# A feed-forward's eleven quads in chunks of 3, 4 and 4 instead of 4, 3 and 4

## The chip, the cores and the metric

The kernel runs on one core of one Trainium2 chip. The time is the device time of the program in microseconds; the time before is the median of three runs.

The engines are called as the profile calls them: PE is the matrix engine TensorE (PEld is its weight load), DVE is VectorE, ACT is ScalarE, POOL is GpSimd, SP is SyncE, which issues most of the loads.

## The reference

One layer for 512 prompt tokens and 32 sample tokens: a feed-forward at half weight, a mixer of two linear attentions, a cross attention, and a second feed-forward at half weight. Only the two feed-forwards matter here:

```python
x = x + 0.5 * _swiglu(_rmsnorm(x, w['ffn1_norm_g']), w['ffn1_w_gate'], w['ffn1_w_up'], w['ffn1_w_down'])
...
x = x + 0.5 * _swiglu(_rmsnorm(x, w['ffn2_norm_g']), w['ffn2_w_gate'], w['ffn2_w_up'], w['ffn2_w_down'])

def _swiglu(x, wg, wu, wd):
    return (jax.nn.silu(x @ wg) * (x @ wu)) @ wd
```

x has 544 rows of 1024; gate and up are 1024 x 2816, down is 2816 x 1024, all in float32.

## The kernel before

**Quads and chunks.** The 2816 hidden columns are 22 blocks of 128. Two blocks m = 0, 1 make a quad, so there are eleven. A list `CHUNKS` (line 340) groups the quads: an entry is the first block of the chunk and its number of quads. In a chunk of nq quads, quad t takes the blocks k0 + t and k0 + t + nq. When a chunk's gates and ups are done, its part of the down product is made and added to x, for four pairs of output blocks.

**Jobs.** `JOBS` (lines 341 to 352) is the list that sets the order of all engines: for each feed-forward and chunk the gate and the up of each quad, then the gate of the next chunk's first quad, then four downs. Before, a feed-forward's 34 jobs are: gate and up of four quads, gate of chunk 1, four downs; up and the rest of chunk 1 (three quads), gate of chunk 2, four downs; up and the rest of chunk 2 (four quads), four downs. Behind the last chunk's ups no gate follows, so its first down stands right behind the up whose result it needs.

**Products.** The first four jobs of a feed-forward (two gates, two ups) are plain matrix products. All others use Strassen's scheme: seven products P1 to P7 instead of eight, on sums and differences of blocks. Each float32 operand is split in a high and a low part, and a product of one block takes three matmuls (high by high, low by high, high by low) of 128 x 128 by 272 columns. Gates and ups have four blocks to sum over in a product (12 matmuls), a down has as many as its chunk has quads: 12 matmuls in a chunk of four, 9 in a chunk of three. `half_size` (line 404) gives this size. `SEQ` is the list of all products in order; P3 of a job comes behind P1 of the next.

**Who makes what for a product.** SP loads a job's five weight blocks into `slots`, ten of them, five a job (lines 548 to 566), as soon as the job two before has been split. Two of the five (issued at line 554, first of the job) get a second block added by a POOL transfer that accumulates (`add_on_load`, line 657); POOL waits for SP's two first. Both kinds are 256 KB, or 192 KB in a down of three quads. ACT copies the high part into `ring_w` (line 845), DVE subtracts it for the low part (line 1325), mostly for two products at once (`GROUPS`). Two products whose sizes differ are not paired, so on the way into and out of a chunk of three quads the splits are single. Behind the split of P1, DVE adds a slot that the POOL transfer must have filled (line 1333), behind that of P2 another (line 1338).

**Results.** DVE and ACT combine the products of gate and up, and DVE makes h of a quad with its sums (lines 1441 to 1454, 1351). ACT and DVE split h into `hs` (lines 886, 889, 1466), in a part for the sums m < 3 and one for the rest. A down's last block waits for the last quad of its chunk (`h_ready`, line 2346):

```python
if j == nk - 1:
    h_ready(NF // 2 * n + (CHUNKS[c][0] // 2 + CHUNKS[c][1] - 1), m)
```

DVE adds a down's results to x (lines 1398, 1409, 1410, 1423, 1437). All PE matmuls of a feed-forward have line 2194, that of their helper.

Of the kernel before, what the change touches and what calls it, by code (L numbers as in the profile page):

```python
# [50 lines left out]
def build(nc, a, o):  # L51

    ctx = ExitStack()
    with ctx:
# [282 lines left out]
        N_PLAIN = 4  # L337
        COMBO = {P1: 0, P2: 2, P3: 1, P4: 6, P5: 3, P6: 5, P7: 4}
        SLOT = {P1: 0, P6: 0, P3: 1, P2: 1, P4: 2, P7: 3, P5: 4, W11: 0, W12: 1, W22: 2, W21: 3}
        CHUNKS = ((0, 4), (8, 3), (14, 4))  # L340
        JOBS = []
        for n in range(2):
            for c, (k0, nq) in enumerate(CHUNKS):
                for t in range(nq):
                    if t or not c:
                        JOBS.append(("gate", n, c, t))
                    JOBS.append(("up", n, c, t))
                if c + 1 < len(CHUNKS):
                    JOBS.append(("gate", n, c + 1, 0))
                JOBS += [("down", n, c, m) for m in range(4)]  # L350
                if c + 1 < len(CHUNKS):
                    pass
# [51 lines left out]
        def half_size(J):  # L404

            return 128 * (CHUNKS[JOBS[J][2]][1] if JOBS[J][0] == "down" else 4)

# [5 lines left out]
        def quad_of(J):  # L413

            return NF // 2 * JOBS[J][1] + CHUNKS[JOBS[J][2]][0] // 2 + JOBS[J][3]

# [85 lines left out]

        LAST_UP = CHUNKS[-1][1] - 1
        mem_k_out = o["mem_k"][0, 0].rearrange("(mb p) h d -> p mb (h d)", p=128)
# [2388 lines left out]
```

## Time and profile before

| | us |
|---|---|
| median of three runs | 1301.96 (1300.91 to 1302.71) |
| the profiled execution | 1297.84 |
| its span, first to last instruction | 1296.0 |
| first feed-forward, jobs of chunk 0's downs to the end of chunk 2's ups | 120.18 to 334.50 |
| PE busy | 1256.2 (97% of the span) |
| DVE busy | 932.5 (72%) |
| ACT busy | 617.1 (48%) |

The profile is of one execution. Its span is that of the core's instructions; the rest of the execution's time lies around it. A row of the timeline gives start, duration, engine, line and operation, and in brackets how long the engine had stood idle before and what ended that. A matmul's duration is longer than the distance to the next one, because they are pipelined; what counts is the distance of their starts. The second feed-forward has the same program as the first.

### The profile page before, as it was taken

The numbers are of one execution on the slowest core, as the hardware profiler recorded it, in microseconds if no ns is written. First come the engines' busy times: TensorE is split into PE (matmuls) and PEld (weight loads), VectorE is DVE, ScalarE is ACT, GpSimd is POOL, SyncE is SP. The second block draws the span as 40 slices with busy tenths as digits, with TensorE's granted clock in tenths as the row PEclk, the third lists the DMA queues.
The fourth block names the chain that finished last, engine by engine and source line by source line (L and its number), as shares of the span: only waits on it lengthen the run. The fifth ranks groups of instructions, "written<-read, shape, count | busy, mean of one in ns | idle before, by whom it ended". The sixth has DMA issues, their size and how long they took to land.

```text
span 1296.0 us, 25334 instructions
## 1 busy us (share of the span) xinstructions
PE 1256.2 (97%) x10321; PEld 1216.5 (94%) x10321; DVE 932.5 (72%) x1326; ACT 617.1 (48%) x962; POOL 196.0 (15%) x184
## 2 busy tenths in 40 slices
PE   7999999999889999999999999999999999999987
PEld 7999999999889999998888899879999999999987
DVE  5988778888793376667766544535698878888885
ACT  6455455555462233345534622324445545645553
POOL 1112222232100000002111000100012222222210
PEclk9999999999899999998999999999999999999988
DMA  6578887888653223324055673541458888798861
GB/s 203 116 158 171 179 171 154 179 189 169 135 118 102 69 80 82 82 82 131 19 132 171 215 244 112 190 176 55 119 124 179 175 177 167 146 199 174 175 125 69
DMA packets 302324, 185.03 MB, mean 143 GB/s; under 512 B 10582, under 2 KB 290368, under 8 KB 302212
## 3 DMA queue, kind: packets, MB, share of 16 engines
q1 hardware_dynamic: 233072, 125.61, 33.8%
q0 software_dynamic: 68976, 57.68, 25.6%
q8 instruction: 81, 1.33, 0.5%
q14 instruction: 31, 0.25, 0.1%
q10 hardware_dynamic: 164, 0.16, 0.0%
HBM read 175.53 MB, written 7.88 MB: 142 GB/s over the span
## 4 chain that ended last, share of the span: by engine, by line
PE 41%; DVE 6%; issue 1%; ACT 1%; DMA 1%; another core or an unknown queue 0%; POOL 0%; SPq 0%; DVEq 0%; ACTq 0%
PE ps L2194 39%; DVE ring_w L1325 2%; PE ps L2697 1%; DMA slots<-in_ffn_w_up 1%; DVE xs_lo L1346 1%; ACT ring_w L845 0%; PE ps L2802 0%; DVE hs L1466 0%; PE ps L2728 0%; DVE hf L1454 0%; DVE hf L1351 0%; DVE xf L1351 0%; DVE hf L1448 0%; DVE xf L1358 0%
## 5 line engine op out<-in xcount | busy, mean ns | idle before, releaser
L2194 PE MATMUL ps<-xs_hi,ring_w 128*128 128x272 f32 x2016 | 382.7, 289 | 3.1 <-DVE ring_w L1325 3.1
L1325 DVE TENSOR_TENSOR ring_w<-slots,ring_w 128x1024 fp32r<-128x1024 f32 (+3 forms) x262 | 273.8, 1046 | 102.3 <-ACT ring_w L845 101.1
L2194 PEld LDWEIGHTS ps<-xs_hi,ring_w 128*128 128x128 f32 x2016 | 316.6, 188 | 3.8 <-DVE ring_w L1325 3.8
L845 ACT ACTIVATE ring_w<-slots 128x1024 fp32r<-128x1024 f32 (+3 forms) x262 | 238.9, 918 | 156.5 <-DVE slots L1333 83.5
L2194 PE MATMUL ps<-xs_lo,ring_w 128*128 128x272 f32 x1008 | 291.7, 289 | 0.0
L2194 PE MATMUL ps<-hs,ring_w 128*128 128x272 f32 x1848 | 242.6, 292 | 10.4 <-DVE hs L1466 7.6
L2194 PEld LDWEIGHTS ps<-hs,ring_w 128*128 128x128 f32 x1848 | 238.3, 192 | 13.0 <-DVE hs L1466 9.0
L2194 PEld LDWEIGHTS ps<-xs_lo,ring_w 128*128 128x128 f32 x1008 | 189.6, 188 | 0.0
L2194 PE MATMUL ps<-xn_hi,w_hi 128*128 128x272 f32 x736 | 155.9, 292 | 1.9 <-DVE w_lo L1290 1.9
L2194 PE MATMUL ps<-xn_hi,w_lo 128*128 128x272 f32 x736 | 153.9, 289 | 0.0
L2194 PE MATMUL ps<-xn_lo,w_hi 128*128 128x272 f32 x736 | 153.4, 288 | 0.0
L784 ACT ACTIVATE w_hi<-raw 128x1024 fp32r<-128x1024 f32 x70 | 73.9, 1056 | 146.6 <-PE ps L2194 146.6
L1290 DVE TENSOR_TENSOR w_lo<-raw,w_hi 128x1024 fp32r<-128x1024 f32 x70 | 85.7, 1225 | 46.7 <-ACT w_hi L784 46.3
L2194 PEld LDWEIGHTS ps<-xn_hi,w_hi 128*128 128x128 f32 x736 | 116.3, 189 | 3.1 <-DVE w_lo L1290 2.2
L2194 PEld LDWEIGHTS ps<-xn_hi,w_lo 128*128 128x128 f32 x736 | 117.0, 190 | 0.0
L2194 PEld LDWEIGHTS ps<-xn_lo,w_hi 128*128 128x128 f32 x736 | 116.2, 189 | 0.0
L2194 PE MATMUL ps<-xe_hi,ring_w 128*128 128x272 f32 x512 | 86.7, 292 | 5.1 <-ACT xe_hi L806 3.2
L657 POOL DMA_DIRECT2D slots<-in_ffn_w_down x48 | 61.5, 1536 | 197.7 <-DMA slots<-in_ffn_w_down 197.7
L868 ACT ACTIVATE parts<-ps 128x272 f32<-128x272 f32 x120 | 47.5, 396 | 91.8 <-PE ps L2194 91.8
L657 POOL DMA_DIRECT2D slots<-in_ffn_w_gate x36 | 46.4, 1552 | 251.9 <-DMA slots<-in_ffn_w_gate 251.9
L2194 PEld LDWEIGHTS ps<-xe_hi,ring_w 128*128 128x128 f32 x512 | 73.4, 191 | 6.0 <-DVE ring_w L1325 5.6
L657 POOL DMA_DIRECT2D slots<-in_ffn_w_up x36 | 46.3, 1547 | 145.7 <-DMA slots<-in_ffn_w_up 145.7
(386 smaller groups left out, 1643.1 us busy)
## 6 DMA issues: line engine op xcount, KB each, us to landing
slots<-in_ffn_w_gate SPq DMA_DIRECT2D x106, 256.0 KB, 3.5
slots<-in_ffn_w_up SPq DMA_DIRECT2D x106, 256.0 KB, 3.5
slots<-in_ffn_w_down SPq DMA_DIRECT2D x80, 256.0 KB, 3.4
raw<-in_w_in SPq DMA_DIRECT2D x30, 512.0 KB, 3.8
slots<-in_ffn_w_gate POOLq DMA_DIRECT2D x36, 256.0 KB, 5.6
slots<-in_ffn_w_up POOLq DMA_DIRECT2D x36, 256.0 KB, 5.5
slots<-in_ffn_w_down POOLq DMA_DIRECT2D x32, 256.0 KB, 5.6
slots<-in_ffn_w_down SPq DMA_DIRECT2D x40, 192.0 KB, 2.7
```

The source lines that it names most:

```text
L657: pool.dma_start(slots[:, b_ + q, 0:128 * nk].rearrange("p (k c) -> p k c", c=128), src, accum_op=ALU.add).then_inc(sem(f"sum_in{J % 2}"), 16)
L784: act.activation(w_hi[u0 % 2][:, :], raw[u0 % 4][:, :], ACT.Copy).then_inc(sem("hi_done"), 1)
L845: act.activation(ring_part(g, 0), sources(g), ACT.Copy).then_inc(sem("prod_hi"), 1)
L868: act.activation(part_of(J, p_), ps[:, x_bank(J), 0:HT], ACT.Copy, scale=-1.0 if p_ == P7 else 1.0)\
L1290: dve.tensor_tensor(w_lo[u0 % 2][:, :], raw[u0 % 4][:, :], w_hi[u0 % 2][:, :].bitcast(F32), ALU.subtract).then_inc(sem("lo_done"), 1)
L1325: dve.tensor_tensor(ring_part(g, 1), sources(g), ring_part(g, 0).bitcast(F32), ALU.subtract)\
L1346: dve.tensor_tensor(xs_lo[:, lo:hi, j, :], xf8[:, lo + 1:hi + 1, :], xs_hi[:, lo:hi, j, :].bitcast(F32), ALU.subtract).then_inc(sem("xs_lo ...
L2194: return pe.matmul(out, lhsT, rhs, start=start, stop=stop, skip_group_check=onto)
L2697: ins = pe.transpose(k_bank(n)[:, k, 128 * mb:128 * mb + 128], kv[K_BUF[b]][:, mb, at_:at_ + 128], ident)
```

## The change

`CHUNKS` gives chunk 0 three quads and chunk 1 four; chunk 2 is the same. All else follows from the list.

```diff
-        CHUNKS = ((0, 4), (8, 3), (14, 4))
+        CHUNKS = ((0, 3), (6, 4), (14, 4))
```

In both kernels jobs 0 to 5 are gate and up of quads 0 to 2, and from job 23 on the jobs are the same (the last up group and downs). Between them: before, gate and up of quad 3, gate of quad 4, four downs of four blocks, ups and gates of quads 4 to 6, gate of quad 7, four downs of three blocks. After: gate of quad 3, four downs of three blocks, ups and gates of quads 3 to 6, gate of quad 7, four downs of four blocks.

DVE around the first down of chunk 0, the rows of the kernel before (hf_98 is the h of a quad, gt the gate, part_101 a product's partial sum):

```order
L1448 TENSOR_TENSOR hf_98<-hf_98,gt 128x816
L1454 TENSOR_TENSOR hf_98<-hf_98 128x544
L1351 SCALAR_TENSOR_TENSOR hf_98<-hf_98 128x272 x2
L1325 TENSOR_TENSOR ring_w<-slots,ring_w 128x2x512
L1333 TENSOR_TENSOR slots<-slots 128x512
L1412 TENSOR_TENSOR gt<-part_101,ps 128x272
L1466 TENSOR_TENSOR hs<-hf_98,hs 128x816
L1325 TENSOR_TENSOR ring_w<-slots,ring_w 128x2x512
L1466 TENSOR_TENSOR hs<-hf_98,hs 128x1088
L1325 TENSOR_TENSOR ring_w<-slots,ring_w 128x2x512
```

DVE at the same place, chunk 0's first down, in the changed kernel:

```order
L1448 TENSOR_TENSOR hf_98<-hf_98,gt 128x816
L1325 TENSOR_TENSOR ring_w<-slots,ring_w 128x384
L1333 TENSOR_TENSOR slots<-slots 128x384
L1454 TENSOR_TENSOR hf_98<-hf_98 128x544
L1351 SCALAR_TENSOR_TENSOR hf_98<-hf_98 128x272 x2
L1325 TENSOR_TENSOR ring_w<-slots,ring_w 128x512
L1412 TENSOR_TENSOR gt<-part_101,ps 128x272
L1466 TENSOR_TENSOR hs<-hf_98,hs 128x816
L1325 TENSOR_TENSOR ring_w<-slots,ring_w 128x2x384
L1466 TENSOR_TENSOR hs<-hf_98,hs 128x1088
L1325 TENSOR_TENSOR ring_w<-slots,ring_w 128x2x384
```

The paired split of 2 x 512 (P1 of the down, P3 of the gate before) became two single ones, of 384 ahead of the sums of h and of 512 behind them. These are the rows that stood at chunk 1's first down before; there the rows above stand now.

POOL's queue of accumulating loads in the first feed-forward, from chunk 0's last up to chunk 1's downs, in the kernel before:

```order
L657 DMA slots<-in_ffn_w_gate 128x4x128 x2
L657 DMA slots<-in_ffn_w_down 128x4x128 x8
L657 DMA slots<-in_ffn_w_up 128x4x128 x2
L657 DMA slots<-in_ffn_w_gate 128x4x128 x2
L657 DMA slots<-in_ffn_w_up 128x4x128 x2
L657 DMA slots<-in_ffn_w_gate 128x4x128 x2
L657 DMA slots<-in_ffn_w_up 128x4x128 x2
L657 DMA slots<-in_ffn_w_gate 128x4x128 x2
L657 DMA slots<-in_ffn_w_down 128x3x128 x8
```

And in the changed kernel:

```order
L657 DMA slots<-in_ffn_w_gate 128x4x128 x2
L657 DMA slots<-in_ffn_w_down 128x3x128 x8
L657 DMA slots<-in_ffn_w_up 128x4x128 x2
L657 DMA slots<-in_ffn_w_gate 128x4x128 x2
L657 DMA slots<-in_ffn_w_up 128x4x128 x2
L657 DMA slots<-in_ffn_w_gate 128x4x128 x2
L657 DMA slots<-in_ffn_w_up 128x4x128 x2
L657 DMA slots<-in_ffn_w_gate 128x4x128 x2
L657 DMA slots<-in_ffn_w_up 128x4x128 x2
L657 DMA slots<-in_ffn_w_gate 128x4x128 x2
L657 DMA slots<-in_ffn_w_down 128x4x128 x8
```

The eight loads of three blocks for the downs stand a gate and an up earlier and those of four blocks come second; SP's queue moves in the same way.

## Rows read from the trace of the kernel before

**Rows 1.** The page: busy time of each engine, and the chain's shares.

```profile
PE 1256.2 (97%) x10321; PEld 1216.5 (94%) x10321; DVE 932.5 (72%) x1326; ACT 617.1 (48%) x962; POOL 196.0 (15%) x184
...
PE 41%; DVE 6%; issue 1%; ACT 1%; DMA 1%; another core or an unknown queue 0%; POOL 0%; SPq 0%; DVEq 0%; ACTq 0%
```

**Rows 2.** Windows of feed-forward one: downs, gates and ups, downs (columns above).

```profile
core 0: us, PE busy (x) PEld busy (x) DVE busy (x) ACT busy (x) POOL busy (x), PEclk, DMA share, GB/s
120.18:164.40 44.22, 44.02 (x350) 43.80 (x349) 36.00 (x49) 22.56 (x32) 10.48 (x9) 1.00 0.84 176
164.40:226.50 62.10, 62.10 (x495) 62.10 (x494) 50.70 (x68) 35.17 (x52) 15.39 (x12) 1.00 0.78 162
226.50:260.70 34.20, 33.94 (x269) 33.72 (x268) 30.12 (x48) 19.17 (x32) 8.30 (x7) 1.00 0.84 181
```

**Rows 3.** Timeline of PE, first downs of chunks 0, 1, 2 (start, us, what).

```profile
120.94 0.54 PE L2194 MATMUL ps<-hs,ring_w 128*128 128x272 f32 x3
121.68 0.65 PE L2194 MATMUL ps<-hs,ring_w 128*128 128x272 f32 x3 [0.20 <-DVE hs L1466]
...
227.00 0.41 PE L2194 MATMUL ps<-hs,ring_w 128*128 128x272 f32 x2
227.67 0.65 PE L2194 MATMUL ps<-hs,ring_w 128*128 128x272 f32 x3 [0.26 <-DVE hs L1466]
...
339.21 1.05 PE L2194 MATMUL ps<-hs,ring_w 128*128 128x272 f32 x3 [3.36 <-DVE hs L1466]
340.84 0.56 PE L2194 MATMUL ps<-hs,ring_w 128*128 128x272 f32 x1 [0.58 <-ACT parts L868]
```

**Rows 4.** Timeline of DVE, before and at the first downs of chunks 0, 1.

```profile
91.47 1.23 DVE L1325 TENSOR_TENSOR ring_w<-slots,ring_w 128x1024 fp32r<-128x1024 f32 x1 [1.60 <-ACT ring_w L845]
...
120.62 1.00 DVE L1466 TENSOR_TENSOR hs<-hf,hs 128x816 fp32r<-128x816 f32 x1
...
218.99 1.23 DVE L1325 TENSOR_TENSOR ring_w<-slots,ring_w 128x1024 fp32r<-128x1024 f32 x1 [1.60 <-ACT ring_w L845]
...
226.62 1.00 DVE L1466 TENSOR_TENSOR hs<-hf,hs 128x816 fp32r<-128x816 f32 x1
```

**Rows 5.** The chain, feed-forward two, behind chunk 1's downs (start, us, what).

```profile
1141.59 0.37 SPq L554
...
1142.00 3.77 DMA slots<-in_ffn_w_up
...
1146.85 5.97 DMA slots<-in_ffn_w_up
...
1155.22 0.45 DVE x L1410
...
1155.81 1.24 PE ps L2194 x8
```

**Rows 6.** Timeline, the load behind chunk 1's downs in both feed-forwards.

```profile
246.78 0.92 SPq L554 DMA_DIRECT2D slots<-in_ffn_w_up  x2
...
257.43 0.69 DVE L1333 TENSOR_TENSOR slots<-slots 128x512 f32<-128x512 f32 x1 [0.44 <-DMA slots<-in_ffn_w_up]
...
1152.91 0.69 DVE L1333 TENSOR_TENSOR slots<-slots 128x512 f32<-128x512 f32 x1 [1.11 <-DMA slots<-in_ffn_w_up]
...
1155.38 0.29 PE L2194 MATMUL ps<-xs_lo,ring_w 128*128 128x272 f32 x1
```

**Rows 7.** Windows behind the last chunk's wait, columns as in rows 2.

```profile
338.00:344.00 6.00, 4.21 (x17) 3.92 (x18) 4.88 (x6) 3.01 (x5) 0.00 (x0) 0.55 0.15 44
344.00:350.00 6.00, 6.00 (x44) 6.00 (x44) 3.21 (x5) 2.35 (x4) 2.57 (x2) 0.88 0.88 185
```

**Rows 8.** Landing times of SP's first loads and POOL's, 60 to 340 us.

```profile
DMA to landing us min/median/max: 2.5/3.3/5.2
DMA to landing us min/median/max: 4.2/5.3/7.9
```

## The prediction

> **What bounds the kernel now.** I read the page's busy times and its chain first: TensorE (PE) is busy for 97% of the span, and work of PE is the largest share of the chain that ended last [rows 1]. So only what makes PE wait, or gives it more or less to do, moves the end. Next I cut the first feed-forward at the borders of its stages [rows 2]. Between 164.40 and 226.50 us PE runs without a gap: 62.10 us for 495 matmuls, which is 62.10 / 495 = 0.1255 us each. A Strassen job of four blocks (7 products x 12 matmuls = 84) therefore takes 84 x 0.1255 = 10.54 us, and a down job of a three-quad chunk (7 x 9 = 63) takes 7.91 us. VectorE (DVE) is busy for 36.00 of 44.22 us (81%) beside the downs of chunk 0 and for 30.12 of 34.20 us (88%) beside the smaller downs of chunk 1 [rows 2]: the smaller job leaves less cover, but DVE still fits.
>
> Then I looked at the places where PE stands still, in PE's own rows. In chunks 0 and 1 there are only two kinds.
>
> First, the first down of a chunk waits for the h of the chunk's last quad, in its last block. In chunk 0, three matmuls start from 120.94, so the next could start at 120.94 + 3 x 0.1255 = 121.32 and starts at 121.68: 0.36 us lost. In chunk 1, two start from 227.00, the next could start at 227.25 and starts at 227.67: 0.42 us lost [rows 3]. The releaser is the same DVE subtraction each time, at 120.62 and 226.62 [rows 4].
>
> Second, the first load after the small downs is late. The weights of the job after chunk 1's downs are loaded by SP and then added to by a POOL transfer. In the second feed-forward the first SP issue stands at 1141.59, SP's pair lands at 1142.00 + 3.77 = 1145.77, POOL's second transfer lands at 1146.85 + 5.97 = 1152.82 [rows 5]. DVE waited 1.11 us for it, so it was ready at 1152.91 - 1.11 = 1151.80: the lead was 10.21 us and the landing took 11.23 [rows 6]. What DVE does next is late, and PE starts at 1155.81 [rows 5] where the matmul before, at 1155.38 [rows 6], allows 1155.51: 0.30 us lost. In the first feed-forward the issue is at 246.78 and DVE was ready at 257.43 - 0.44 = 256.99: again a lead of 10.21 us, a wait of 0.44 us, and no loss on PE [rows 6]. So about 0.8 us of such a wait is covered (1.11 costs 0.30, 0.44 costs nothing).
>
> **The change part by part.** Each part occurs in both feed-forwards; I cost one and double it.
>
> PE's work. Chunk 0's four downs go from 12 to 9 matmuls a product: 4 x 7 x 3 = 84 matmuls less, 84 x 0.1255 = -10.54 us. Chunk 1's four downs go from 9 to 12: +10.54 us. One gate job and one up job (the fourth quad) move from before chunk 0's downs to before chunk 1's, with their loads and DVE work. The sum on PE is 0. The bytes loaded are equal too: in either order four jobs of a feed-forward load 7 x 192 KB instead of 7 x 256 KB, and SP's and POOL's queues hold the same transfers with the 192 KB group earlier.
>
> The wait at the first down. The order rows show DVE's work around chunk 0's first down turning, row by row, into what stands at chunk 1's first down before (single splits of 384, then the first hs subtraction). So chunk 0 should lose 0.42 us where it lost 0.36, and chunk 1 should lose 0.36 where it lost 0.42: +0.06 and -0.06, sum 0. This holds if DVE reaches the new place in the same state as the old one. The new first down is the fourth job after the plain ones, close to the place where DVE is behind and PE waits for it. The row that decides is the split of the second pair of products in the gate job ahead of the downs: at 91.47 DVE has stood idle 1.60 us before it, waiting for ScalarE, and at 218.99, the same place ahead of chunk 1, also 1.60 us [rows 4]. DVE has caught up by then, so I take no lag. From both sides: the wait can shrink by at most 0.42 us, and if the first down met DVE in the state of the last chunk, where no gate job stands between up and down, it would lose far more, 3.36 + 0.58 us [rows 3]; the gate job still stands between here, so I take the near row.
>
> The late load. The small downs now stand in chunk 0, and the same late load should follow them there, ahead of chunk 1's first up: nothing in the first feed-forward, 0.30 us in the second. Chunk 1's downs become full ones, and behind chunk 0's full downs no such wait showed: PE was busy for 62.10 of 62.10 us [rows 2]. Taken away 0.30, put back 0.30, sum 0. Below, it is gone in both places: -0.30 us. Above, from the longest landings seen in this feed-forward, 5.2 us for SP's and 7.9 us for POOL's transfer [rows 8]: with 0.41 us between SP's two issues, 0.3 to POOL's start and 0.8 between its two, 0.4 + 5.2 + 0.3 + 0.8 + 7.9 = 14.6 us, less the lead of 10.21 and the 0.8 that is covered = 3.6 us a feed-forward. I take the middle value because the two places of before are the same job sequence.
>
> A rule is to be weighed here. In the trace the two transfers that follow each other take 3.77 and 5.97 us [rows 5]. The Trainium skill, "DMA: Bandwidth & Descriptors", section "Anatomy of one DMA — SWDGE (gpsimd) path", fits a transfer as some 2.0 us fixed plus bytes over 436 GB/s, which is an estimate of 2.6 us for 256 KB. By it the pair with its issues would land some 6.7 us after the first issue, no load would be late anywhere, and the sum would be -0.3 us; the trace disagrees with it here, and the measurement decides.
>
> What does not move. The last chunk keeps its four quads, its jobs follow in the same order, and its long wait of 3.36 us [rows 3] stays, with the low clock behind it [rows 7].
>
> **Sum.** The profiled execution took 1297.84 us with a span of 1296.0. PE's work -10.54 + 10.54, first downs +0.06 - 0.06, late loads -0.30 + 0.30: 0 in each feed-forward, so 1297.84 again. The median of the three runs is 1301.96, 4.12 us above the profiled one; carried over, the forecast is **1302.0**. What a measurement of this kernel can tell from no change is about 0.2%, 2.6 us.
>
> **The rivals.**
>
> Loads in time. With half the chunk behind it, the queue may be emptier at the new place, and the job after the small downs gets its sums in time: -0.30 us, 1301.7. For it speaks the DMA share of 0.78 in the gate and up stage [rows 2]; against it, that the share was 0.84 beside the downs of either chunk and the lead of 10.21 us comes from PE's pace alone. (The fit of the Trainium skill's page above would also have them in time.)
>
> Loads late, the side on which the change costs. At the new place the loads are issued just after the backlog behind the plain jobs; if SP's and POOL's transfers run into each other there, the landing takes up to 14.6 us. To cost 2.6 us, each feed-forward must lose 0.15 + 1.3 = 1.45 us, so both landings must take over 10.21 + 0.8 + 1.45 = 12.5 us; halfway to the bound, +3.5 us, gives 1305.5. A lesser lateness, up to that point, gives 1302.3 to 1304.6. Against it: two such landings took 10.6 and 11.23 us. Were PE to stop as long as at the last chunk's wait, the clock could fall as well, as it does there.
>
> The clock. After PE's stop of 3.36 us the granted clock of 338 to 344 is 0.55 and of 344 to 350 is 0.88 [rows 7]: the lower level of 1.2 GHz for part of it, where 2.4 is full. That is 6 x 0.45 + 6 x 0.12 = 3.4 us of clock, of which PE stood still for 1.2 + 0.6 us and lost nothing: some 2.5 us of cost, as far as these rows tell. If the shifted stages let the clock stand in both feed-forwards, 5.0 us go, 1297.0; one more such stretch costs 2.5 and gives 1304.5 or more. The stop itself does not change, so I give either little.
>
> That the change does not do what it says is out: the order rows show the 3-block loads moved.
>
> **How the numbers follow.** Exchange without a rest, 1302.0: 0.62. Loads in time, 1301.7: 0.14. Loads somewhat late, up to 1304.6: 0.12. Loads late in both, 1305.5: 0.06. Clock kept, 1297.0: 0.04. Clock lost once more: 0.02. Faster by over 0.2%: 0.04. Within: 0.62 + 0.14 + 0.12 = 0.88. Slower: 0.06 + 0.02 = 0.08. The three runs lie 1.05 us below to 0.75 above their median; since three understate the spread I take 1.75 times that, 1.84 and 1.31. Low end: 1301.96 - 0.30 - 1.84 = 1299.8. High end: 1301.96 + 1.31 + 1.3, the somewhat late loads at half their way, = 1304.6. Outside lie the last three cases and a little of the third.
>
> **What would show it.** Right: two stages of about 34.2 and 44.2 us in the other order, a PE gap of 0.4 us at each first down, and DVE waiting 0.4 to 1.1 us for a load after chunk 0's downs and nowhere after chunk 1's. Wrong: a PE gap of over 1 us behind chunk 0's small downs, DVE without its idle time before the first down, or a stretch of lower clock where there was none.

## The result, and the profile after

The changed kernel takes 1303.92 us (median of 20 runs, 1300.32 to 1307.80); the kernel before, on the same chips, 1300.95 (20 runs, 1298.12 to 1302.72). The ratio is 1.0024, 95% interval 1.0016 to 1.0033: 3.1 us slower, from 2.1 to 4.3. The time is inside the range of the forecast, but no change was forecast, with 0.08 for slower by over 0.2%, and slower by over 0.2% is what came. The runs also lie further apart than those of before.

The profiled execution of the changed kernel took 1302.41 us with a span of 1300.5, against 1297.84 and 1296.0. Its page, to be held against [rows 1]: the same instructions, and PE busy 4.5 us longer (where is said below, at the windows of the whole program).

```profile
PE 1260.7 (97%) x10321; PEld 1220.9 (94%) x10321; DVE 932.8 (72%) x1326; ACT 617.0 (47%) x962; POOL 196.0 (15%) x184
```

The windows of the first feed-forward, cut as in [rows 2] (same columns): the small downs now come first, then ups and gates, then the full downs.

```profile
99.68:135.94 36.26, 34.08 (x269) 33.66 (x268) 29.75 (x48) 20.27 (x34) 9.19 (x8) 1.00 0.80 170
135.94:219.21 83.27, 83.27 (x659) 83.27 (x660) 70.24 (x91) 45.57 (x68) 20.94 (x17) 1.00 0.85 178
219.21:263.43 44.22, 44.02 (x351) 43.80 (x350) 35.84 (x48) 22.58 (x33) 11.00 (x9) 1.00 0.86 178
```

The full downs take 44.22 us as before. The small ones take 36.26 where they took 34.20: 2.06 us more, for the same 269 matmuls. PE's timeline says where. Its first downs of chunks 0 and 1 (as in [rows 3]), and the end of chunk 0's small downs:

```profile
99.68 0.92 PE L2194 MATMUL ps<-hs,ring_w 128*128 128x272 f32 x6
100.85 0.52 PE L2194 MATMUL ps<-hs,ring_w 128*128 128x272 f32 x2 [0.26 <-DVE hs L1466]
...
133.73 0.29 PE L2194 MATMUL ps<-xs_lo,ring_w 128*128 128x272 f32 x1
135.94 1.36 PE L2194 MATMUL ps<-hs,ring_w 128*128 128x272 f32 x9 [1.93 <-DVE x L1410]
...
219.21 1.04 PE L2194 MATMUL ps<-hs,ring_w 128*128 128x272 f32 x7
220.46 0.64 PE L2194 MATMUL ps<-hs,ring_w 128*128 128x272 f32 x3 [0.20 <-DVE hs L1466]
```

From 133.73 the next matmul could start at 133.86 and starts at 135.94: 2.08 us lost. The chain of waits through that place (start, us, what), where [rows 5] had 3.77 and 5.97 for the two landings:

```profile
119.94 0.37 SPq L554
...
120.35 4.86 DMA slots<-in_ffn_w_up
...
125.50 0.78 POOL slots L657
126.28 6.68 DMA slots<-in_ffn_w_up
...
135.36 0.45 DVE x L1410
...
135.94 1.11 PE ps L2194 x7
```

And DVE's timeline at three jobs behind downs (compare [rows 6]): behind the small downs of the first feed-forward, behind the full downs of its chunk 1 (259.85), and behind the small downs of the second feed-forward.

```profile
129.00 1.15 DVE L1325 TENSOR_TENSOR ring_w<-slots,ring_w 128x384 fp32r<-128x384 f32 x2
133.05 0.69 DVE L1333 TENSOR_TENSOR slots<-slots 128x512 f32<-128x512 f32 x1 [2.90 <-DMA slots<-in_ffn_w_up]
...
259.85 0.69 DVE L1333 TENSOR_TENSOR slots<-slots 128x512 f32<-128x512 f32 x1
...
1030.14 0.69 DVE L1333 TENSOR_TENSOR slots<-slots 128x512 f32<-128x512 f32 x1 [0.53 <-DMA slots<-in_ffn_w_up]
```

So the late load moved to chunk 0, as said, and in the first feed-forward it is far later than it was anywhere before: 13.02 us from the first issue (119.94) to the last landing (132.96), where the two places of before had 10.56 and 11.23. In the second feed-forward the same job had its loads after 10.65 us, and PE did not stop.

What else differs between the two profiles is read from windows of the whole program: ahead of the first matmul of the feed-forward, first feed-forward, middle, second feed-forward, rest.

```profile
0.00:15.66 15.66, 8.37 (x53) 7.86 (x54) 4.68 (x9) 7.89 (x13) 3.59 (x10) 1.00 0.93 286
15.66:342.06 326.40, 318.48 (x2497) 316.74 (x2497) 274.06 (x367) 181.71 (x259) 71.99 (x56) 0.99 0.77 161
342.06:916.02 573.96, 562.36 (x4886) 527.27 (x4886) 342.93 (x533) 224.80 (x402) 43.33 (x58) 0.98 0.42 122
916.02:1239.36 323.34, 318.00 (x2497) 316.66 (x2497) 268.90 (x356) 174.71 (x248) 71.98 (x56) 0.99 0.77 161
```

The same cuts in the kernel before give 14.95, 324.26, 572.97 and 322.21 us. The first feed-forward is 2.14 us longer. The start, the middle and the second feed-forward are longer by 0.71, 0.99 and 1.13 us, the rest is 0.47 shorter. A second profile of each kernel (below) shows the 2.14 again, and it shows the start and the second feed-forward to come and go. The middle is longer in the second pair too. There PE does the same 4886 matmuls in 562.36 us of busy time instead of 559.71, at a mean granted clock of 0.98 instead of 0.99: at a lower clock a matmul takes longer, and these 2.65 us are more than half of the 4.5.

### The profile page after: what moved, and what is told of

It reads as the page before. It is cut to its first block, busy times and chain, and to the rows that moved or that the text cites. A ratio compares the mean times of both kernels' runs of the same rounds, so it can differ in the third digit from the quotient of the medians.

```text
span 1300.5 us, 25334 instructions
## 1 busy us (share of the span) xinstructions
PE 1260.7 (97%) x10321; PEld 1220.9 (94%) x10321; DVE 932.8 (72%) x1326; ACT 617.0 (47%) x962; POOL 196.0 (15%) x184
## 4 chain that ended last, share of the span: by engine, by line
PE 76%; DVE 15%; ACT 4%; issue 3%; DMA 1%; another core or an unknown queue 0%; POOL 0%; SPq 0%; DVEq 0%; ACTq 0%
PE ps L2194 73%; DVE ring_w L1325 3%; DVE xs_lo L1346 1%; ACT ring_w L845 1%; PE ps L2697 1%; DMA slots<-in_ffn_w_up 1%; DVE hs L1466 1%; DVE hf L1454 1%; DVE lv_qk L1657 1%; DVE hf L1351 1%; DVE xf L1351 0%; PE ps L2802 0%; DVE hf L1448 0%; DVE xf L1358 0%; DVE xf L1360 0%
```

## Experiments

Two theories. **Instruction theory**: a transfer of 16 KB that brings PE its own next instructions falls into the left loads (SP's first pair, line 554) of the job behind the small downs; any other job has slack for it, this one has none (the kernel before has such a load at 306.27 us: a transfer 2.4 us behind the issue, 5.08 us for the second load, and neither DVE nor PE waited for it). **Chance theory**: the late load was one bad execution and the 3 us lie elsewhere, say in the clock. The trace showed the first theory's transfer in the stretch between the pair's first issue and its last landing (119.94 to 125.21 us, the view of DMA queues), as the one packet of queue 8 (packets, MB, share of 16 engines):

```profile
## 3 DMA queue, kind: packets, MB, share of 16 engines
q1 hardware_dynamic: 2040, 1.02, 66.8%
q0 software_dynamic: 137, 0.06, 9.8%
q8 instruction: 1, 0.02, 1.2%
```

1.2% of 16 engines over 5.27 us is 1.0 us of one engine.

### Both kernels once more

No edit in either.

> The changed kernel once more, unaltered, for a second profiled execution. Instruction theory (a 16 KB transfer of TensorE's own instructions falls into the loads of the job behind chunk 0's downs of the first feed-forward, and that job has no slack): the transfer stands again within 3 us of 122.4 us in the span, the second left load again takes over 4.5 us, the slot sum of line 1333 is again over 2 us late near 130 us, and TensorE again stops for 1.5 to 2.5 us near 134 us; 1303 to 1304.5 us. Chance theory (the late load was one bad execution, and the 3 us lie in the clock): the chain of loads takes 10.3 to 11.5 us this time, TensorE loses under 1 us there, and the time is 1303 to 1304.5 us all the same.

> The kernel before once more, unaltered: a second profiled execution, and a comparison of the kernel with itself. Both theories: ratio 1.0000, its interval within 0.9990 to 1.0010. Instruction theory: the jobs behind its three-quad downs (near 250 and 1150 us) again have their sums at most 1.2 us late, since no instruction transfer falls into their left loads, and TensorE loses at most 0.6 us at each. Chance theory: lateness there differs from the first profile by over 1 us in one of the two.

Measured: changed kernel 1.0020 (1.0008 to 1.0031) of the kernel before; the kernel before against itself 1.0004 (0.9993 to 1.0014). The changed kernel's median, 1302.13 us, lies under the 1303 to 1304.5 expected; the kernel before took 1300.19 beside it. Each one's second profile, first feed-forward and middle (changed, then before):

```profile
15.78:342.19 326.41, 318.70 (x2498) 316.81 (x2498) 273.93 (x367) 181.69 (x259) 71.99 (x56) 0.99 0.77 161
342.19:915.48 573.29, 562.51 (x4885) 527.51 (x4885) 342.86 (x533) 224.93 (x402) 43.32 (x58) 0.98 0.42 122
```

```profile
15.85:340.11 324.26, 318.27 (x2497) 316.75 (x2497) 274.08 (x367) 181.78 (x259) 72.01 (x56) 0.99 0.77 162
340.11:911.95 571.84, 559.11 (x4885) 523.97 (x4885) 342.66 (x533) 224.82 (x402) 43.43 (x58) 0.99 0.42 122
```

326.40 and 326.41 against 324.26 and 324.26. The chain at the late job was 13.02 us again, the transfer stood 2.5 us behind the first issue again (2.4 the first time), PE stopped 1.92 us. In the kernel before the same job took 10.43 us this time (10.56). The chance theory falls for the first feed-forward. The second feed-forward took 322.14 and 321.78 us, so most of the 1.13 us more of the first pair of profiles was not the change's. The middle, 573.29 against 571.84 us, is 1.45 us longer this time; what that can mean is said with the clock, further down.

### The change in one feed-forward only

The list was given a second level, one entry for each feed-forward.

```diff
-        CHUNKS = ((0, 3), (6, 4), (14, 4))
+        CHUNKS = (((0, 3), (6, 4), (14, 4)), ((0, 4), (8, 3), (14, 4)))
```

The other kernel has the two entries exchanged.

> Chunks of 3, 4 and 4 in the first feed-forward, 4, 3 and 4 in the second. Instruction theory: the whole cost is in the first feed-forward (2.09 us at the job behind chunk 0's downs, 0.4 us won back at chunk 1): +2 to +3.3 us, ratio 1.0015 to 1.0027. Clock theory: half of the cost, +1 to +2 us, ratio 1.0008 to 1.0015.

> Chunks of 4, 3 and 4 in the first feed-forward, 3, 4 and 4 in the second. Instruction theory: the second feed-forward showed a chain of loads of 10.65 us and no stop of TensorE there, against 0.30 us lost before: -0.4 to +0.4 us, ratio 0.9997 to 1.0003. Clock theory: half of the cost, +1 to +2 us, ratio 1.0008 to 1.0015.

Measured: first feed-forward alone 1.0024 (1.0012 to 1.0036), second alone 1.0000 (0.9987 to 1.0013). By the medians the whole cost is in the first; the two intervals alone would just allow a half in each, but the first feed-forward took 326.33 us with the first changed and 324.53 with the second. The profile of the one with the second changed is not that quiet, though: PE stopped 2.32 us behind its small downs, which was not expected, in an execution 2 us above that kernel's median. So in the second feed-forward the late load comes in some of the profiles; in the first it was there in every profile that had the small downs first and no added instructions.

### Other addresses

Behind the small downs the changed kernel loads columns from block 6 on, the kernel before from block 14 on. Here the chunks exchange weights (the quad numbers follow by count).

```diff
-        CHUNKS = ((0, 3), (6, 4), (14, 4))
+        CHUNKS = ((0, 3), (14, 4), (6, 4))
```

> Chunks of 3, 4 and 4 as changed, but the second and third chunk exchange the weights they read: the job behind chunk 0's small downs loads columns from block 14 on, as the one behind the three-quad downs of the kernel before does, and not from block 6 on. Instruction theory: the same as the changed kernel, chain of loads 12.5 to 13.5 us at that job of the first feed-forward, TensorE stopped 1.6 to 2.3 us, ratio to before 1.0015 to 1.0035. Address theory: chain 10.3 to 11.2 us, stop under 0.6 us, ratio 0.9990 to 1.0010.

Measured: 1.0028 (1.0014 to 1.0041); chain 14.25 us, PE stopped 3.16 us, the transfer 2.8 us behind the issue. The address is not the cause. Chain and stop are above the 12.5 to 13.5 and 1.6 to 2.3 us expected, so the instruction theory did not give their size; here the load ahead was late as well (2.0 us into the pair, in the table below).

### A semaphore of its own for each added load

If the cost is the sum's wait and nothing else, it goes when the sum waits only for what it reads. Line 1333 reads the slot of the first POOL load, yet its semaphore counted both. ScalarE's split of P5 reads the same slot and gets the same semaphore. Two semaphores used once each later in the kernel were merged with neighbours to make room (not shown).

```diff
-    accum_op=ALU.add).then_inc(sem(f"sum_in{J % 2}"), 16)
+    accum_op=ALU.add).then_inc(sem(f"sum{q}_in{J % 2}"), 16)
...
-    act.wait_ge(sem(f"sum_in{J % 2}"), 32 * ((nth(J) + 1) // 2))
+    act.wait_ge(sem(f"sum{4 if p_ == P5 else 3}_in{J % 2}"), 16 * ((nth(J) + 1) // 2))
...
-    dve.wait_ge(sem(f"sum_in{J % 2}"), 32 * ((nth(J) + 1) // 2))
+    dve.wait_ge(sem(f"sum4_in{J % 2}"), 16 * ((nth(J) + 1) // 2))
```

> The changed kernel with a semaphore for each of the two adding loads on POOL's queue, so that the sum of line 1333 waits for the first of them alone (it reads only that one's slot), and the split of P7 for the second. In the profile of the changed kernel the first landed at 129.89 us, the second at 132.96, VectorE was free at 130.15. Late-load theory (the whole cost is this sum's wait): the sum starts within 0.3 us of VectorE being free, TensorE's stop of 1.92 us goes or falls under 0.5 us, and the kernel takes 1.5 to 2.2 us less than the changed kernel: ratio to before 0.9997 to 1.0012. If instead the second load is needed almost as early by the split of P7, a stop of 1 to 2 us moves to the product of P7 and the ratio stays 1.0012 to 1.0030.

> The kernel before with the same two semaphores. In its profile the sum behind the three-quad downs was 0.44 and 1.11 us late, which cost TensorE nothing and 0.30 us. Late-load theory: 0 to 0.5 us faster, ratio 0.9995 to 1.0003. Where it costs elsewhere (the waits on merged semaphores later in the kernel): up to 1.0010.

> The kernel before with the two semaphores, the same file as in the earlier run, for a narrower interval: 0.9988 [0.9975, 1.0001] there. Late-load theory: its profile had no stop of TensorE behind the three-quad downs, where the kernel before had lost 0 and 0.30 us, so at most 0.5 us of gain, ratio 0.9995 to 1.0003. If the gain of the first run is real, 0.9980 to 0.9995.

Measured: changed kernel with it 0.9993 (0.9983 to 1.0004) of the kernel before; kernel before with it 0.9988 (0.9975 to 1.0001), and measured again 0.9996 (0.9987 to 1.0005), so that the first of the two, below the range expected, was not confirmed. The changed kernel's DVE and PE at the late job, and its first feed-forward:

```profile
130.51 0.69 DVE L1333 TENSOR_TENSOR slots<-slots 128x512 f32<-128x512 f32 x1 [0.33 <-DMA slots<-in_ffn_w_up]
...
133.75 0.29 PE L2194 MATMUL ps<-xs_lo,ring_w 128*128 128x272 f32 x1
133.88 1.28 PE L2194 MATMUL ps<-hs,ring_w 128*128 128x272 f32 x9
```

```profile
15.66:339.92 324.26, 318.32 (x2497) 316.67 (x2497) 274.14 (x367) 181.73 (x259) 71.99 (x56) 0.99 0.77 163
```

The chain was no shorter (13.94 us, left load 5.27), but the sum waited 0.33 us and PE went from 133.75 to 133.88 without a stop; the first feed-forward took 324.26 us, to the hundredth what the kernel before takes. That settles what costs in the first feed-forward: the wait for the second load, 2.14 us. All three intervals hold 1, so nothing here is for certain a better kernel than the one before.

### Moving the instruction transfers

What makes the load late in the first place? The page of the changed kernel counts the instruction transfers (number, MB, share of 16 engines):

```profile
q8 instruction: 81, 1.33, 0.4%
```

81 for PE's 10321 matmuls and as many weight loads: one for 255 instructions, semaphore waits not counted. If the transfers go by PE's place in its program, more instructions at the start bring each later one earlier against the loads. The edit, with 64, 192 and 256 waits on a long satisfied semaphore:

```diff
+            for _ in range(64):
+                pe.wait_ge(sem("const_in"), 16)
             for i in range(N_PROD):
```

> The changed kernel with 64 waits added to TensorE's program ahead of its first feed-forward matmul, all on a semaphore that is long satisfied, at a place where TensorE idles 3.0 us. TensorE's instruction transfers come 256 of its instructions (some 16 us) apart, so 64 more instructions put every later one about 4 us earlier against the loads: the one at 122.4 us goes to about 118.5, ahead of the left loads of the job behind chunk 0's downs (119.9 to 125.2 us). Instruction theory: there the second left load takes 3.2 to 4.0 us instead of 4.9, the chain of loads 10.3 to 11.6 us instead of 13.0, TensorE stops for at most 0.7 us instead of 1.9, and the kernel takes 1.2 to 2.2 us less than the changed kernel (ratio to before 1.0000 to 1.0012, less what of the waits the idle time does not hide, which shows as a later first matmul). In the second feed-forward the transfer at 1030.0 goes to about 1026, into the same job's slower queue: a stop of 0 to 1 us there. Address theory (the weight columns that this job now reads are slow) and position theory (this place behind small downs is slow whatever the transfer does): the chain again takes 12.5 to 13.5 us, TensorE stops 1.5 to 2.3 us, ratio 1.0015 to 1.0035.

Measured: 1.0039 (1.0025 to 1.0052); chain 12.94 us, stop 1.85 us, the transfer 2.6 us behind the issue. It decides nothing: in the trace two waits stand in one instruction, so that 32 were added, and the transfer of the first feed-forward did not move. (In the second feed-forward others moved, and PE stopped there too, 2.10 us.)

> The changed kernel with 192 added waits at the place of the 64 before. The 64 had become 32 instructions (two waits go into one), a quarter of what was meant, and had moved the transfer at 122.4 us by nothing; 192 make 96 instructions, some 6 us of TensorE's stream, so the request that came near 121 us comes near 115 us against the loads, in the middle of the third small downs and not in the left loads of the job behind them. The measure is the first feed-forward alone, from its first matmul to the end of its last long stop: 326.40 us in both profiles of the changed kernel, 324.26 in both of the kernel before; it leaves the start out, which the added waits make some 3 us later. Instruction theory: second left load 3.2 to 3.7 us after its issue instead of 4.9, chain of loads 10.3 to 11.8 us instead of 13.0, TensorE's stop at most 0.8 us instead of 1.92, first feed-forward 324.3 to 325.2 us. Position theory (any job behind small downs at this place is late, the transfer lies there by accident): left load 4.5 to 5.2 us, chain 12.5 to 13.5, stop 1.6 to 2.3, first feed-forward 326.0 to 327.0 us.

> The same with 256 added waits, 128 instructions, half of the distance between two transfers (some 8 us). Instruction theory: in the first feed-forward the request moves to about 113 us, again out of that job's left loads: chain 10.3 to 11.8 us, stop at most 0.8 us, first feed-forward 324.3 to 325.2 us. In the second, the transfer that stood 10.6 us behind the issue of the same job's left loads moves to about 2.6 us behind it, into them: left load 4.1 to 5.2 us, stop 1.0 to 2.5 us, second feed-forward 323.0 to 325.0 us against 321.8 to 322.2 without a stop. Position theory: both places as in the changed kernel, first feed-forward 326.0 to 327.0 us, second 322.0 to 323.5 us.

Measured: 1.0077 (1.0063 to 1.0090) and 1.0115 (1.0097 to 1.0132), of which the late start is the most: the first matmul of the feed-forward stood at 21.53 and 25.16 us instead of 15.66. With 192, the late job of the first feed-forward: landing of its left pair, the queues between issue and landing, and DVE.

```profile
DMA to landing us min/median/max: 2.9/3.1/3.3
```

```profile
## 3 DMA queue, kind: packets, MB, share of 16 engines
q1 hardware_dynamic: 1184, 0.59, 54.8%
q0 software_dynamic: 166, 0.08, 17.3%
```

```profile
135.66 0.69 DVE L1333 TENSOR_TENSOR slots<-slots 128x512 f32<-128x512 f32 x1 [0.42 <-DMA slots<-in_ffn_w_up]
...
1036.18 0.69 DVE L1333 TENSOR_TENSOR slots<-slots 128x512 f32<-128x512 f32 x1 [3.84 <-DMA slots<-in_ffn_w_up]
```

No packet of queue 8 is in the pair any more (the transfer came 2.4 us ahead of it), the second load took 3.3 us instead of 4.9, the sum was 0.42 us late, PE did not stop, and the first feed-forward took 323.44 us. That is below the 324.3 to 325.2 expected and below the 324.26 of the kernel before; the later start, which gives the other engines time, may be why, and no run separates it. It did not empty the queue ahead of the pair: POOL's load of the job ahead landed 2.0 us into it, later than in the changed kernel (1.2). In the second feed-forward of the same execution it went the other way: a transfer now stood 3.2 us behind the issue, the load took 4.95 us, the sum was 3.84 us late and PE stopped 2.86 us. With 256 the same twice: 3.54 us and no stop in the first feed-forward; a transfer 2.8 us behind the issue, as expected, 4.91 us and a stop of 1.83 us in the second. Its feed-forwards took 323.32 and 325.38 us, expected were 324.3 to 325.2 and 323.0 to 325.0.

The job behind the small downs in all profiles (us). The pair is SP's first two loads, line 554, and the chain runs from its first issue to the landing of POOL's second load. The transfer's start is counted from the pair's first issue, and of the transfers from 4 us ahead of it to 9 us behind the nearest is given; "ahead" is when POOL's last load of the job ahead landed, counted likewise; PE's stop is the idle time of its row in the timeline:

| kernel, feed-forward | transfer | ahead | second left load | chain | PE stop |
|---|---|---|---|---|---|
| before, 1 / 2 | -3.3 / 5.3 | 1.4 / 1.5 | 3.39 / 3.77 | 10.56 / 11.23 | 0 / 0.14 |
| before again, 1 / 2 | -3.6 / 5.3 | 1.4 / 1.2 | 3.30 / 3.36 | 10.43 / 10.70 | 0 / 0 |
| changed, 1 / 2 | 2.4 / -3.6 | 1.2 / 1.3 | 4.86 / 3.28 | 13.02 / 10.65 | 1.93 / 0 |
| changed again, 1 / 2 | 2.5 / -3.5 | 1.6 / 1.5 | 4.90 / 3.49 | 13.02 / 11.22 | 1.92 / 0.12 |
| first only, 1 / 2 | 2.5 / 5.4 | 1.4 / 1.0 | 4.96 / 3.40 | 12.98 / 10.81 | 1.88 / 0 |
| second only, 1 / 2 | -3.7 / 7.3 | 1.3 / 2.2 | 3.43 / 4.50 | 10.53 / 13.42 | 0 / 2.32 |
| addresses, 1 / 2 | 2.8 / none | 2.0 / 1.8 | 5.46 / 3.61 | 14.25 / 11.31 | 3.16 / 0.21 |
| 64 waits, 1 / 2 | 2.6 / 7.2 | 1.3 / 2.6 | 4.99 / 4.41 | 12.94 / 13.19 | 1.85 / 2.10 |
| 192 waits, 1 / 2 | -2.4 / 3.2 | 2.0 / 1.2 | 3.28 / 4.95 | 10.54 / 13.96 | 0 / 2.86 |
| 256 waits, 1 / 2 | 8.0 / 2.8 | 1.6 / 1.3 | 3.54 / 4.91 | 10.88 / 12.93 | 0 / 1.83 |
| changed, two semaphores, 1 / 2 | 2.8 / none | 1.7 / 1.9 | 5.27 / 4.36 | 13.94 / 13.22 | 0 / 0 |
| before, two semaphores, 1 / 2 | -2.8 / 5.1 | 1.8 / 1.3 | 3.30 / 3.49 | 10.70 / 10.64 | 0 / 0 |
| before, two semaphores, again, 1 / 2 | -3.0 / 5.5 | 2.3 / 0.9 | 4.42 / 3.51 | 12.71 / 10.87 | 0 / 0 |

In all eight places of the table where the transfer starts 2.4 to 3.2 us behind the issue, the load takes 4.86 us or more. Moving it away from the pair, with nothing else edited at that job, made the load normal both times; moving it into the pair made the load late, once where that was forecast (256 waits) and once where it was not (192). So the position theory, by which the job is late wherever the transfer lies, falls.

Over all 780 such pairs of the thirteen profiles (60 in each) it holds too, with a limit. Of the 617 whose job ahead was done within 1.7 us, the 33 with a transfer starting 0.5 to 2.3 us behind the issue all took 4.1 to 5.2 us; the 475 with none from 0.5 to 3.3 us behind it had a median of 3.35, and six of them took over 4.1. In between, from 2.3 to 3.3, there are two groups: the gates' and ups' loads took 3.2 to 3.9 us or 4.6 to 5.4, as the transfer came behind or ahead of the pair's own packets, it seems; the trace view does not tell the order on one engine. So behind the full downs of the kernel before a transfer 3.07 us behind the issue (146.12) left the load at 3.29 us, and the same holds in six of the seven places behind full downs where it came 3.0 to 3.3 us behind; the seventh, with 256 waits, took 5.00. Why a transfer of 1.0 us makes a load 1.6 us longer was not tried either.

Four places of the table are late without it. There POOL's last load of the job ahead landed 1.9 to 2.6 us into the pair; it was 0.9 to 2.0 where the load was normal, so the two ranges meet. In the changed kernel small downs follow each other every 8 us (issues at 103.77, 111.99, 119.94) and take 9.2 us to load, so a delay in one reaches the next. That fits, and was not tried by itself. The last row also shows the two semaphores at work in the kernel before: a chain of 12.71 us that cost no stop.

## Why the prediction was half right

**The number: inside the range, in part by luck.** The forecast stands on the median of three runs, 1301.96 us, 1.0 above the median of twenty, 1300.95. Set about that, the same range would end at 1303.6, and 1303.92 was measured. And of the signs that the prediction named for being wrong, the first came: a PE gap of over 1 us behind chunk 0's small downs.

**Exchange of PE's work: right.** 44.22 us for the full downs as before, 34.20 + 2.06 for the small ones.

**First downs: right.** Chunk 0: six matmuls from 99.68, next possible at 100.43, started at 100.85, 0.42 us lost. Chunk 1: seven from 219.21, next possible at 220.09, started at 220.46, 0.37 lost. Forecast 0.42 and 0.36. DVE had its 1.60 us of idle time in the gate job ahead of the new first down:

```profile
92.18 1.23 DVE L1325 TENSOR_TENSOR ring_w<-slots,ring_w 128x1024 fp32r<-128x1024 f32 x1 [1.60 <-ACT ring_w L845]
```

**The late load: the step that failed.** The prediction said: the late load follows the small downs to chunk 0 and costs there what it cost at chunk 1, nothing in the first feed-forward and 0.30 us in the second, "because the two places of before are the same job sequence". It did follow, and nothing was late behind chunk 1's full downs. The working of its lateness was right too: DVE was ready at 133.05 - 2.90 = 130.15, 10.21 us behind the issue, the lead of before; with a landing of 13.02 and 0.8 us of cover that is 2.0 us, and 2.06 to 2.14 were measured. Only the size of the landing was taken from the wrong rows. The same job sequence does not make the same landing time: what lay in the queue beside it at 122.4 us, an instruction transfer, was in no row that I had read, and in the left loads of the two places of before there was none, in either profile. The row that should have widened the centre was [rows 8]: SP's loads ranged up to 5.2 us and POOL's to 7.9, and a job with 0.8 us of slack beyond the lead can meet that range anywhere. The 5.08 us at 306.27 us, one of the longest in that row, was itself a load with a transfer in it. The rival "loads late" named place, mechanism and bound (14.6 us, 3.6 a feed-forward); it deserved far more than 0.18, and the part for one feed-forward alone, 2 to 3 us, more than the part for both.

**The rule on landing times: the measurement decides.** By the fit of the Trainium skill, "DMA: Bandwidth & Descriptors", section "Anatomy of one DMA — SWDGE (gpsimd) path", no load would be late anywhere; the late chain took 13.02 us, and the shortest in any row of the table 10.43. The section fits transfers that GpSimd issues; POOL's second one took 6.68 us here, where the fit gives an estimate of 2.6.

**The clock: a cost that can come behind the stop.** The prediction gave little to a clock that falls after a longer stop. In the two profiles of the changed kernel it did not fall behind the late load: the granted clock is 1.00 in the window that begins at 135.94, and in the second profile from 135 to 138. But of the nine stops of 1.8 to 3.2 us in the table, it fell behind six. In the kernel with the second feed-forward changed (columns of the windows as before, PEclk third from the end):

```profile
1029.00:1032.00 3.00, 0.86 (x4) 0.89 (x5) 2.93 (x5) 2.27 (x3) 2.24 (x2) 0.87 0.26 64
1032.00:1035.00 3.00, 3.00 (x16) 3.00 (x16) 2.97 (x6) 0.63 (x1) 0.33 (x1) 0.57 1.36 206
```

PE stopped until 1031.14; then the clock was at its lower level, 1.2 of 2.4 GHz, for part of both windows: 3 x 0.13 + 3 x 0.43 = 1.7 us. Behind the stop of 3.16 us (other addresses) it was twice that. So a stop of some 2 us can cost 1.7 us more. Together with a stop in the second feed-forward now and then this would fit the wider spread of the changed kernel's runs, and the 1.0 us by which the median's 3.1 exceeds the 2.14 of the profiles.

The middle is another candidate for that 1.0 us: it is 1.0 and 1.5 us longer at a lower mean clock in the two pairs of profiles. It took 573.07 to 573.16 us also with the first feed-forward alone changed, with other addresses and with 64 waits, in which PE stopped behind the small downs of the first feed-forward, and 572.12 and 571.89 with the second alone changed and with two semaphores in the changed kernel, in which it did not. But the kernel before with two semaphores took 573.68 and 573.78, and the kernels with 192 and 256 waits 573.81 and 575.25, without such a stop. So whether a stop in the first feed-forward lowers the clock of the middle stays open, and how often each comes in the runs without a profile is not known.

What remains of the forecast: the last chunk's stop stayed (3.36 us), and in the first feed-forward all parts but one came to zero.

## What to carry to other kernels

Before an order of loads is moved, compute for each consumer how far its loads lead it, and compare that with the longest landing of such a load in the trace, not with the landing at the place that looks alike; a job without slack can turn a disturbance of the queue into a stop of the bound engine. Let a consumer wait for the transfer that it reads and not for a semaphore that counts its neighbour too: in the profile that alone took the 2.14 us away, with the loads as late as ever. When the slow place has the same instructions as a fast one, look at what else is in the queues between issue and landing.

## What the runs showed of the hardware

PE's own instructions come by DMA beside the kernel's data: the page counts them among the core's 16 DMA engines, in 81 transfers of 16 KB, one per 255 matmuls and weight loads, some 16 us apart in the feed-forwards, each about 1.0 us on one engine. One that starts 2.4 us behind the issue of a pair of 256 KB loads made the second load 4.9 us instead of 3.3, and with the POOL loads chained to it the whole took 13.0 us instead of 10.5. They follow PE's position in its program (96 more instructions ahead brought one from 2.4 us behind the issue to 2.4 us ahead of it), and in the first feed-forward the same load was hit in all three profiles with these chunks there and no other edit (122.4, 122.6 and 122.7 us). An edit that only reorders work can move the hit: in the kernel before the nearest transfer started 3.3 and 3.6 us ahead of the pair. In the second the transfer stood 3.6 and 3.5 us ahead of that load in the two executions of the changed kernel, and 7.3 to 7.7 us ahead with other addresses, with two semaphores and with the second alone changed; what sets that was not tried.

The Trainium skill, "Runtime: NRT & Kernel Launch", section "Instruction fetch mechanics", says that instructions are refilled in blocks of 16 KiB, 256 of them, over a DMA queue of the sequencer's own, and that the cost of a crossing is "mostly hidden". The count here agrees (255, semaphore waits left out), and no idle time of PE at the late job was put down to a block; the price was paid by the load beside it.

PE's count alone does not set the start: 32 more instructions left the one at 122 us where it was, 96 moved it. Why was not tried.
